# Feed-forward projections of a two-layer trunk: six equal matmuls per weight tile against five of unequal length

## What is computed

```python
x += 0.5 * SwiGLU_a(RMSNorm(x));  x += Mixer(RMSNorm(x));  x += 0.5 * SwiGLU_b(RMSNorm(x))

def swiglu(x, w_gu, w_down):            # w_gu 1024 x 5632, w_down 2816 x 1024
    a, b = jnp.split(x @ w_gu, 2, axis=-1)
    return (jax.nn.silu(a) * b) @ w_down
```

## Time and profile before

| quantity | value |
|---|---|
| device time, median of three runs | 2580.63 us (2578.86 to 2581.56) |
| profiled execution, span from first to last instruction | 2571.9 us |
| TensorE busy | 2477.0 us (96%) |
| TensorE weight loads busy | 2384.1 us (93%) |
| VectorE / ScalarE / GpSimd busy | 1270.5 / 565.3 / 1680.7 us |
| mean granted TensorE clock | 0.981 |

### The profile page before, as it was taken

The page is one execution under the profiler, slowest core; times in us unless marked ns, Lnnn a source line. Parts: engine busy times, 40 slices in busy tenths (PEclk is TensorE's granted clock), DMA queues, the critical chain, the costliest instruction groups (busy, mean ns, idle before and its releaser), DMA issues.

```text
span 2571.9 us, 52956 instructions
## 1 busy us (share of the span) xinstructions
PE 2477.0 (96%) x20047; PEld 2384.1 (93%) x20047; DVE 1270.5 (49%) x2226; ACT 565.3 (22%) x848; POOL 1680.7 (65%) x750
## 2 busy tenths in 40 slices
PE   7999998998799899999999999999999899999997
PEld 7999998997577899999999999999999799999996
DVE  4444335787533654443344443367767644444433
ACT  3222101004733222220022220012222211222101
POOL 5777775664413477777777777765555367777773
PEclk9999999998899899999999999999999999999998
DMA  4333333895465333333323333233433333333331
GB/s 121 96 93 91 99 90 85 276 317 175 123 213 185 98 88 93 90 96 90 116 83 90 91 95 101 81 93 113 123 101 109 111 90 90 90 91 92 99 95 56
DMA packets 472391, 291.20 MB, mean 113 GB/s; under 512 B 32785, under 2 KB 438411, under 8 KB 472270
## 3 DMA queue, kind: packets, MB, share of 16 engines
q1 hardware_dynamic: 407286, 221.15, 29.6%
q10 hardware_dynamic: 64992, 68.54, 8.4%
HBM read 273.50 MB, written 16.23 MB: 113 GB/s over the span
## 4 chain that ended last, share of the span: by engine, by line
PE 86%; DVE 7%; ACT 3%; POOL 1%; issue 1%; ACTq 1%; DMA 0%; SPq 0%; DVEq 0%; POOLq 0%
PE ACC L807 76%; PE ACC L1075 2%; PE ACC L1044 1%; PE ACC L1317 1%; PE ACC L1327 1%; POOL WLO L716 1%; DVE TB L2318 1%; DVE RMOL L2257 0%; DVE XL L1784 0%; DVE SSR L2235 0%; PE ACC L1329 0%; PE ACC L1142 0%; POOL WHI L713 0%; ACT TAP L1497 0%; PE ACC L901 0%
## 5 line engine op out<-in xcount | busy, mean ns | idle before, releaser
L713 POOL TENSOR_TENSOR WHI<-RAW,ZERO 128x1024 fp32r<-128x1024 f32 (+1 forms) x341 | 691.5, 2028 | 665.0 <-PE ACC L807 625.8
L716 POOL TENSOR_TENSOR WLO<-RAW,WHI 128x1024 fp32r<-128x1024 f32 (+1 forms) x341 | 915.1, 2683 | 49.3 <-POOL WHI L713 2.3
L807 PE MATMUL ACC<-XH,WHI 128*128 128x260 f32 x4032 | 821.6, 285 | 4.2 <-DVE XL L1784 1.9
L807 PE MATMUL ACC<-XH,WLO 128*128 128x260 f32 x4032 | 812.8, 283 | 0.0
L807 PE MATMUL ACC<-XL,WHI 128*128 128x260 f32 x4032 | 811.1, 283 | 0.0
L807 PEld LDWEIGHTS ACC<-XH,WHI 128*128 128x128 f32 x4032 | 624.1, 189 | 22.9 <-DVE PRJ L1871 6.1
L807 PEld LDWEIGHTS ACC<-XH,WLO 128*128 128x128 f32 x4032 | 621.8, 189 | 0.0
L807 PEld LDWEIGHTS ACC<-XL,WHI 128*128 128x128 f32 x4032 | 620.5, 188 | 0.0
L807 PE MATMUL ACC<-HH,WHI 128*128 128x260 f32 x1408 | 284.1, 283 | 1.1 <-POOL WLO L716 1.1
L807 PE MATMUL ACC<-HH,WLO 128*128 128x260 f32 x1408 | 283.1, 282 | 0.0
L807 PE MATMUL ACC<-HL,WHI 128*128 128x260 f32 x1408 | 282.5, 282 | 0.0
(11 more groups left out here) (395 smaller groups left out, 2373.6 us busy)
## 6 DMA issues: line engine op xcount, KB each, us to landing
RAW<-in_ffn_w_gu SPq DMA_DIRECT2D x176, 512.0 KB, 3.8
RAW<-in_ffn_w_down SPq DMA_DIRECT2D x64, 704.0 KB, 4.7
KPAGES<-in_cache_fox_k ACTq DMA_DIRECT2D x128, 256.0 KB, 4.1
RAW<-in_c_w_in SPq DMA_DIRECT2D x48, 512.0 KB, 3.9
VPAGES<-in_cache_fox_v SPq DMA_DIRECT2D x72, 256.0 KB, 3.6
RAW<-in_ab_w_in SPq DMA_DIRECT2D x28, 512.0 KB, 5.7
VPAGES<-in_cache_fox_v ACTq DMA_DIRECT2D x56, 256.0 KB, 3.3
SSR<-in_state_ret_S ACTq DMA_DIRECT2D x8, 1024.0 KB, 6.6
```

The costliest lines, as they stand in the source:

```text
L713: pool.tensor_tensor(WHI[:, slot, 0:nk, :], RAW[:, slot, 0:nk, :], ZERO[:, :].broadcast_to([P, nk, P]), ALU.add).then_inc(hi_split, 1)
L716: pool.tensor_tensor(WLO[:, slot, 0:nk, :], RAW[:, slot, 0:nk, :], WHI[:, slot, 0:nk, :].bitcast(F32), ALU.subtract).then_inc(split, 1)
L807: ins = pe.matmul(ACC[acc][:, n, 0:HALF], w[:, slot, k, :], a[:, k0 + k, n * HALF:(n + 1) * HALF], start=first and opens, stop=final and c ...
```

## The change

The 520 tokens are parted at 282 (`LEFT`) instead of 260. High and low parts of a chunk now lie behind each other in one tile (`XS`, `HS`): 520 high values, then 520 low values. The low values are rotated: first those of the right 238 tokens (`RIGHT`), then those of the left 282. So the right tokens' high values and their low values are one contiguous run of 476.

`multiply` issues five matmuls per chunk: WHI x left high (282 columns), WHI x right high and right low together (476), WHI x left low (282), WLO x left high (282), WLO x right high (238). The joint matmul writes two separate sums into one bank, `right` (columns 0 to 237) and `right_low` (238 to 475), and these are added later. In the up projections ScalarE copies `right_low` out of the accumulator into `LOWS` (the tile `SQ`, idle there) and VectorE adds it to `right` before it scales. In the down projections VectorE adds `right`, `left` and `right_low` to `X` with three instructions. The subtraction that makes `HL`, and the one that makes `XL` ahead of an up projection (norms 0, 2, 3 and 5), become two each, for the rotation. The projections into and out of the mixers keep six matmuls of 260; `down_halves` is the old `down` under a new name.

```diff
@@ -31,6 +31,8 @@
 SEQ, DEC = 512, 8
 TOK = SEQ + DEC
 HALF = TOK // 2
+LEFT = 282
+RIGHT = TOK - LEFT
...
@@ -189,13 +191,13 @@
         WLO = new("WLO", [P, 2, KH, P], F32R)
 
         cursor["xs"] = cursor["main"]
-        XH = new("XH", [P, KD, TOK], F32R, "xs")
-        XL = new("XL", [P, KD, TOK], F32R, "xs")
+        XS = new("XS", [P, KD, 2, TOK], F32R, "xs")
+        XH, XL = XS[:, :, 0], XS[:, :, 1]
...
-        HH = new("HH", [P, KF, TOK], F32R, "h")
-        HL = new("HL", [P, KF, TOK], F32R, "h")
+        HS = new("HS", [P, KF, 2, TOK], F32R, "h")
+        HH, HL = HS[:, :, 0], HS[:, :, 1]
...
+
+        LOWS = SQ[:, 0:2 * RIGHT].rearrange("p (j t) -> p j t", j=2)
+
+        def left(acc):
+            return ACC[acc][:, 0, 0:LEFT]
+
+        def right(acc):
+            return ACC[acc][:, 1, 0:RIGHT]
+
+        def right_low(acc):
+            return ACC[acc][:, 1, RIGHT:2 * RIGHT]
...
+        lows_ready = sem("lows_ready")
+        lows_added = sem("lows_added")
+        right_added = sem("right_added")
...
@@ -791,6 +808,27 @@
 
         @block.tensor
         def _(pe):
+            def multiply(acc, slot, k, pair, chunk, opens, closes):
+
+                w_hi, w_lo = WHI[:, slot, k, :], WLO[:, slot, k, :]
+                row = pair[:, chunk].rearrange("p j t -> p (j t)")
+                pe.matmul(left(acc), w_hi, row[:, 0:LEFT], start=opens, stop=False)
+                pe.matmul(ACC[acc][:, 1, 0:2 * RIGHT], w_hi, row[:, LEFT:LEFT + 2 * RIGHT], start=opens, stop=False)
+                pe.matmul(left(acc), w_hi, row[:, LEFT + 2 * RIGHT:], start=False, stop=False)
+                pe.matmul(left(acc), w_lo, row[:, 0:LEFT], start=False, stop=closes)
+                return pe.matmul(right(acc), w_lo, row[:, LEFT:TOK], start=False, stop=closes)
+
+            def project_by_parts(unit, slot, nk, acc, pair, k0=0, last=True, ready=None, late=None):
+
+                hold(pe, split, unit + 3)
...
+                    ins = multiply(acc, slot, k, pair, k0 + k, k == 0 and k0 == 0, last and k == nk - 1)
+                ins.then_inc(used, 1)
...
-                    for w, a, opens, closes in ((WHI, XH, True, False), (WHI, XL, False, False), (WLO, XH, False, True)):
-                        for n in range(2):
-                            ins = pe.matmul(ACC[0][:, n, 0:HALF], w[:, 0, k, :], a[:, k, n * HALF:(n + 1) * HALF],
-                                            start=k == 0 and opens, stop=k == KD - 1 and closes)
+                    ins = multiply(0, 0, k, XS, k, k == 0, k == KD - 1)
                 ins.then_inc(used, 1)
-                project(1, 1, KD, 1, XH, XL)
+                project_by_parts(1, 1, KD, 1, XS)
                 pe.wait_ge(tile_free, KD + 4)
                 statistics(0)
-                project(2, 0, KD, 2, XH, XL)
+                project_by_parts(2, 0, KD, 2, XS)
                 pe.wait_ge(std_ready, 1)
-                project(3, 1, KD, 3, XH, XL)
+                project_by_parts(3, 1, KD, 3, XS)
...
                             pe.wait_ge(std_ready, r + 1)
-                        project(u0 + 4 * i + s, (u0 + s) % 2, KD, s, XH, XL, ready=(xl_ready, KD * r + 1))
...
@@ -873,7 +908,7 @@
                 with pe.Fori(1, KF // 2) as i:
                     two_pairs(i)
 
-            def down(name, hi, lo, nk, per_chunk, ready, late=None):
+            def down_halves(name, hi, lo, nk, per_chunk, ready, late=None):
...
+            def down(name, pair, nk, per_chunk, ready, late=None):
+                u0, t0 = unit_at[name], tile_at[name]
+                with pe.Fori(0, KD // 2) as i:
+                    for s in range(2):
+                        hold(pe, tile_free, t0 + 2 * i + s + 3)
+                        for m in range(per_chunk):
+                            n = per_chunk * s + m
+                            project_by_parts(u0 + 2 * per_chunk * i + n, (u0 + n) % 2, nk, s, pair, k0=nk * m,
+                                             last=m == per_chunk - 1, ready=ready, late=late)
...
-            down("down0", HH, HL, KH, 2, (h_ready, 1))
+            down("down0", HS, KH, 2, (h_ready, 1))
...
@@ -1410,14 +1455,24 @@
                                scale=1.0 / D_MODEL).then_inc(std_ready, 1)
 
             def up(f, logf_count=0):
-                t0 = tile_at[f"up{f}"]
-                with act.Fori(0, KF) as j:
-                    hold(act, tile_free, t0 + 2 * j + 5)
-                    act.activation(TA[:, :], TA[:, :], ACT.Silu).then_inc(act_ready, 1)
-                    hold(act, hfull_ready, KF * f + j + 1)
-                    act.activation(HH[:, bass.ds(j, 1), :].rearrange("p a t -> p (a t)"), TH[:, :], ACT.Copy).then_inc(hh_ready, 1)
-                    if logf_count:
-                        load_logf(logf_count * j, logf_count)
+                t0, u0 = tile_at[f"up{f}"], unit_at[f"up{f}"]
+
+                def copy_lows(tile, acc):
+
+                    hold(act, used, u0 + tile + 3)
+                    hold(act, lows_added, 2 * KF * f + tile + 1)
+                    act.activation(LOWS[:, acc % 2, :], right_low(acc), ACT.Copy).then_inc(lows_ready, 1)
+
+                with act.Fori(0, KF // 2) as i:
+                    for s in range(2):
+                        copy_lows(4 * i + 2 * s, 2 * s)
+                        hold(act, tile_free, t0 + 4 * i + 2 * s + 5)
+                        act.activation(TA[:, :], TA[:, :], ACT.Silu).then_inc(act_ready, 1)
+                        copy_lows(4 * i + 2 * s + 1, 2 * s + 1)
...
+                        act.activation(HH[:, bass.ds(2 * i + s, 1), :].rearrange("p a t -> p (a t)"), TH[:, :], ACT.Copy).then_inc(hh_ready, 1)
+                        if logf_count:
+                            load_logf(2 * logf_count * i + logf_count * s, logf_count)
...
@@ -1781,11 +1836,12 @@
                 hold(dve, ssq_ready, SSQ_STEPS * r + d + 1)
                 dve.tensor_tensor(SSQ[:, :], SSQ[:, :], SQ[:, :], ALU.add).then_inc(ssq_ready, 1)
...
-                dve.scalar_tensor_tensor(out=XL[:, bass.ds(d, 1), :].rearrange("p a t -> p (a t)"),
-                                         in0=X[:, bass.ds(d, 1), :].rearrange("p a t -> p (a t)"),
-                                         scalar=PAR[:, bass.ds(PAR_NORM + KD * r + d, 1)],
-                                         in1=XH[:, bass.ds(d, 1), :].rearrange("p a t -> p (a t)").bitcast(F32),
-                                         op0=ALU.mult, op1=ALU.subtract).then_inc(xl_ready, 1)
+                low, high = (a[:, bass.ds(d, 1), :].rearrange("p a t -> p (a t)") for a in (XL, XH))
+                x = X[:, bass.ds(d, 1), :].rearrange("p a t -> p (a t)")
+                for to, of in ((slice(0, RIGHT), slice(LEFT, TOK)), (slice(RIGHT, TOK), slice(0, LEFT))) if r in BY_PARTS else ((slice(0, TOK),) * 2,):
+                    ins = dve.scalar_tensor_tensor(out=low[:, to], in0=x[:, of], scalar=PAR[:, bass.ds(PAR_NORM + KD * r + d, 1)],
+                                                   in1=high[:, of].bitcast(F32), op0=ALU.mult, op1=ALU.subtract)
+                ins.then_inc(xl_ready, 1)
...
+            def update_by_parts(name, scale, turn, per_chunk=2):
+
...
+                        hold(dve, used, u0 + per_chunk * d + per_chunk + 2)
+                        xd = X[:, bass.ds(d, 1), :].rearrange("p a t -> p (a t)")
+                        dve.scalar_tensor_tensor(out=xd[:, LEFT:TOK], in0=right(s), scalar=scale, in1=xd[:, LEFT:TOK],
+                                                 op0=ALU.mult, op1=ALU.add).then_inc(right_added, 1)
+                        dve.scalar_tensor_tensor(out=xd[:, 0:LEFT], in0=left(s), scalar=scale, in1=xd[:, 0:LEFT],
+                                                 op0=ALU.mult, op1=ALU.add)
+                        hold(dve, right_added, KD * turn + d + 1)
+                        dve.scalar_tensor_tensor(out=xd[:, LEFT:TOK], in0=right_low(s), scalar=scale, in1=xd[:, LEFT:TOK],
+                                                 op0=ALU.mult, op1=ALU.add).then_inc(tile_free, 1)
+                        norm_chunk(r, d)
...
@@ -1807,25 +1881,32 @@
 
             def up(f):
                 t0, u0 = tile_at[f"up{f}"], unit_at[f"up{f}"]
+
+                def scaled(out, tile, acc):
+
+                    hold(dve, used, u0 + tile + 3)
+                    dve.tensor_tensor(out[:, 0:LEFT], left(acc), RSTD[:, 0:LEFT], ALU.mult)
+                    hold(dve, lows_ready, 2 * KF * f + tile + 1)
+                    dve.tensor_tensor(right(acc), right(acc), LOWS[:, acc % 2, :], ALU.add).then_inc(lows_added, 1)
+                    hold(dve, lows_added, 2 * KF * f + tile + 3)
+                    dve.tensor_tensor(out[:, LEFT:TOK], right(acc), RSTD[:, LEFT:TOK], ALU.mult).then_inc(tile_free, 1)
+
                 with dve.Fori(0, KF // 2) as i:
                     for s in range(2):
...
-                        hold(dve, used, u0 + 4 * i + 2 * s + 3)
```

(14 more changed lines are left out.)

37 lines of the change are left out of this document (26 added, 11 removed).

## The result

The changed kernel takes 2591.28 us (median of 20 runs, 2583.03 to 2599.94); the kernel before took 2579.89 beside it (20 runs, 2572.82 to 2584.0). The ratio is 1.0045, 95% interval 1.0034 to 1.0055: slower, by some 11 us. 2508 was forecast, with a chance of 0.86 for faster.

A forecast was written before the change was run, and what follows sets the result against it. TensorE's back-to-back matmuls were taken to bound the kernel. Matmuls -84 us, uneven edges +6, X update +2.6, XL +1.3 and +0.6, up to down +1.3 gave -72: 2580.6 - 72 = 2508 us, range 2492 to 2572.

The forecast's parts named there:

- What bounds the kernel: Whole kernel: TensorE, busy in 96% of the span, sets the time; only matmuls following each other faster can win any.
- What 120 ns consists of: TensorE's inner loop: a matmul takes the greater of a 120.1 ns weight-load floor and N / 2.4 + 2.5 ns.
- a fixed cost that is paid at both clocks: Rival, TensorE's inner loop: 11.8 ns per matmul, one of six goes, 25 us less 6, 2562 us; chance 0.14.
- Sum of the matmuls: Inner loop of up and down projections: 681.2 ns a chunk against 721, 84 us less over 2112 chunks.
- slow-columns rival: Inner loop: fp32r columns take 0.462 ns each, 721 ns a chunk with five matmuls or six, 2587 us; chance 0.11.
- XL at the load: At the load, making XL in two adds up to 1.2 us; half taken because ScalarE shares the path, 0.6.
- Update of X: End of each down projection: three VectorE instructions for one, 0.65 us more, four times, 2.6 us.
- XL in two: Before norms 2, 3 and 5: 0.15 us more, and TensorE waits 0.28 longer at chunk 7; three times 0.43, 1.3 us.
- Up to down: From up to down projection: TensorE's wait for GpSimd's split grows from 0.27 to 0.6 us; four times 0.32, 1.3 us.
- VectorE and ScalarE: Up projections: about 1.2 us more VectorE work per pair, 6.2 us in 10.9, hidden behind TensorE's other accumulators: nothing.

The follow-up runs named there:

- lengths: Computation left out, only matmuls timed, 16 in a row per length of 64 to 512 columns: fp32r 111.6 ns at 128, 118.7 at 260, 131.0 at 282.

## Why the prediction was wrong

**What bounds the kernel.** Right: TensorE's inner loop sets the time, and its change shows in the result. The loss is small, though, and more than half of it comes from the edges (below).

**What 120 ns consists of.** This is the step that failed. The prediction took "120.1 ns for `fp32r`, whose loads the trace shows at no other pace" as the floor of a weight load and forecast "the greater of that floor and N / 2.4 + 2.5 ns". The floor is 111.6 (lengths) and the 120.1 are 260 columns of a stream that runs at about 0.435 ns a column. The rows with plain float32 were read rightly: the floor they show, 101 to 112, agrees with the 111.6. The error was to lift it to 120.1 rather than leave 8 ns unexplained. The low clock rightly excluded a fixed cost that is paid at both clocks, but can't show a limit that lies between the two clocks. That sentence stood in the prediction, beside the rival "the columns themselves are fed more slowly", and got a chance of 0.11.

**Sum of the matmuls.** Forecast 681 ns a chunk, measured 723: -84 us became about +5.5 (1408 times 2.5 ns and 704 times 3 ns). The slow-columns rival said 721, and 220 ns behind the 476-run (measured 218.5). It came within 5 us of the time, 2587, in part by luck: it had nothing for the chunks (5.4 us measured) and 6 for the edges. What it lacked is the 7 ns (estimate) that a matmul costs besides, given back once per chunk, and that the runs of this parting take some 8 ns a chunk more than the line and the floor.

**XL at the load.** Forecast 0.6. TensorE's first unit of up0 ended 1.8 us later (29.66 for 27.89). But over the seven executions with this `XL` in two it ended between 27.89 and 29.68, 28.9 on average, and in the three without at 27.73 to 28.11. So the 1.8 is in part chance, and the cost is about 1 us on average.

**Update of X.** Forecast 0.65 us at each down projection. Measured 0.38, and 0.33 to 0.34 where a mixer follows. After down3 the three take 1.09 us (2569.56 to 2570.65), for 0.71: the pieces overlap, so that their lengths don't add. But the `statistics` behind them slowed. Timeline of TensorE before, and a window there (busy PE, PEld, DVE, ACT, POOL, then PEclk, DMA share, GB/s):

```profile
2547.61 1.14 PE L816 MATMUL ACC<-SSQ,ONES 128*128 128x260 f32 x4 [2.56 <-DVE SSQ L1782]
```

```profile
2547.60:2548.70 1.10, 1.09 (x4) 0.68 (x4) 0.75 (x1) 1.06 (x1) 0.00 (x0) 1.00 0.00 0
```

The same two views after:

```profile
2572.35 2.10 PE L854 MATMUL ACC<-SSQ,ONES 128*128 128x260 f32 x4 [2.96 <-DVE SSQ L1837]
```

```profile
2572.30:2574.50 2.20, 2.10 (x4) 1.18 (x4) 0.76 (x1) 1.10 (x2) 0.00 (x0) 0.50 0.00 0
```

Behind a wait of 2.96 us the four records ran at the low level, behind 2.56 at the high one. Of the two runs at 264 one lost 1.9 us behind down3 and the other 0.5, so the longer wait doesn't bring it every time.

**XL in two.** Forecast 0.43 more, so 1.08 with the update. Measured from down1 to up2: X starts at 1305.33, chunk 7 at 1311.09, 5.76 us, for 1291.71 - 1286.48 = 5.23. 0.53, half of it. At up1 and up3, where `XL` in two comes without the update in parts, the first unit took 0.15 us more: the added instruction alone. The other 0.28 was to come from a faster TensorE. It waited 0.87 us ahead of up2's chunk 7, for 1.5 forecast.

**Up to down.** Forecast 0.32 us each for a shorter unit. The unit is not shorter, and at three of four places the tie costs under 0.1 us (8.47 us against 8.43). At down0 it costs 3.2, from VectorE, which the prediction had excluded.

**VectorE and ScalarE.** "Nothing" was right in up1 to up3: TensorE's units there are even at 5.787 us. It was wrong at the end of up0. The prediction also had up0's DMA issues behind the copy on ScalarE, but the next copy stands behind them. The working added up durations (6.2 us of work in 10.9) and took a VectorE instruction's length for its own, although 1820 ns for `HL` beside 641 for ScalarE's copy of the same size was a sign that it stood waiting.

**Together.** Steady chunks 5.4 us, up0 to down0 3.2, the load 1.8, the tail 1.9, the other first units 1.0: 13.3 by the profiles. With 0.7 at the mixers' first units and 1.4 in retention it is 15.4, against 11.4 by the medians; the load and the tail differ by 1.5 us and more from one execution to the next.

## What to carry to other kernels

Before a tuned inner loop is re-cut by instruction length, the pace has to be known at three lengths at least: one short micro kernel gave in one run what the whole trace of one length couldn't. The parting itself is worth a scan in small steps: 264 or 272 for 282 turned a loss of 0.45% into a gain of 0.3%. Where a cost stands above a known floor, the remainder belongs to something, and a low-clock stretch tells only that it doesn't bind there. A sum of busy times says an engine has room; whether an instruction is late depends on what it is caught behind.
